# Moving the high and low parts of the weights by 16 and 48 bytes in SBUF

## The reference

```
proj = hn @ w_in[l]
h = h + jnp.concatenate([o_attn, o_rec], axis=-1) @ w_out[l]
g, u = jnp.split(hn @ w_gu[l], [D_FF], axis=-1)
h = h + (jax.nn.silu(g) * u) @ w_down[l]
```

## Time and profile before

| | |
|---|---|
| time, median of 3 runs | 1700.67 us (1699.19 to 1701.57) |
| span of the profiled execution | 1705.6 us |
| mean granted TensorE clock in it | 0.982 |
| TensorE busy | 1619.8 us, 95% |
| weight loads busy (beside TensorE) | 1418.1 us, 83% |
| VectorE busy | 1017.1 us, 60% |
| ScalarE busy | 869.4 us, 51% |
| moved by DMA | 253.94 MB, mean 149 GB/s |

### The profile page before, as it was taken

One profiled execution on the slowest core, in us unless ns is written; L12 is line 12 of the kernel. 1 busy time (PEld: TensorE's weight loads), 2 busy tenths in 40 slices (PEclk: granted clock), 3 DMA queues, 4 the chain that ended last, 5 costly groups with the idle time before them and its releaser, 6 DMA issues.

```text
span 1705.6 us, 28040 instructions
## 1 busy us (share of the span) xinstructions
PE 1619.8 (95%) x11794; PEld 1418.1 (83%) x11794; DVE 1017.1 (60%) x1577; ACT 869.4 (51%) x1467; POOL 21.1 (1%) x38
## 2 busy tenths in 40 slices
PE   6999999989989999999989999999999898999997
PEld 6968999989779999887758778888888674789997
DVE  7675545465855455725465765425556776687676
ACT  6754434448545344534565553324444647666563
POOL 0000000000000000310000000000000000000000
PEclk9999999999999999999999999999999999999999
DMA  7365445353555463772201452232213520154532
GB/s 295 135 231 217 169 152 200 137 194 139 201 214 205 147 232 130 221 229 78 74 1 70 178 198 101 85 128 95 83 68 133 198 100 25 73 208 156 220 144 92
DMA packets 60524, 253.94 MB, mean 149 GB/s; under 512 B 4976, under 2 KB 8304, under 8 KB 42480
## 3 DMA queue, kind: packets, MB, share of 16 engines
q1 hardware_dynamic: 59088, 249.01, 39.6%
q0 software_dynamic: 1312, 3.15, 1.0%
HBM read 251.09 MB, written 1.05 MB: 148 GB/s over the span
## 4 chain that ended last, share of the span: by engine, by line
PE 83%; DVE 9%; ACT 6%; issue 2%; DMA 1%; SPq 0%; DVEq 0%; ACTq 0%
PE PA L910 63%; PE PA L970 4%; DVE WL_t L1550 2%; PE PB L851 2%; PE PB L1320 2%; PE PA L998 2%; PE PB L1307 1%; ACT WH_t L2277 1%; PE PA L946 1%; PE PA L947 1%; PE PA L952 1%; PE PA L865 1%; PE PA L1504 1%; PE PB L1250 1%; DMA raw<-in_w_ada 1%
## 5 line engine op out<-in xcount | busy, mean ns | idle before, releaser
L910 PE MATMUL PA<-XH_t,WH_t 128*128 128x256 f32 (+2 forms) x1984 | 629.6, 317 | 4.9 <-DVE XL_t L1746 2.4
L1550 DVE TENSOR_TENSOR WL_t<-raw,WH_t 128x1024 fp32r<-128x1024 f32 (+1 forms) x344 | 444.5, 1297 | 312.0 <-ACT WH_t L2277 311.6
L910 PE MATMUL PA<-XL_t,WH_t 128*128 128x256 f32 (+2 forms) x1984 | 624.1, 315 | 0.0
L910 PE MATMUL PA<-XH_t,WL_t 128*128 128x256 f32 (+2 forms) x1984 | 623.8, 314 | 0.0
L2277 ACT ACTIVATE WH_t<-raw 128x1024 fp32r<-128x1024 f32 (+1 forms) x344 | 380.8, 1111 | 155.2 <-PE PA L910 139.7
L910 PEld LDWEIGHTS PA<-XH_t,WH_t 128*128 128x128 f32 x1984 | 376.8, 190 | 34.5 <-issue 7.9
L910 PEld LDWEIGHTS PA<-XH_t,WL_t 128*128 128x128 f32 x1984 | 376.9, 190 | 21.6
L910 PEld LDWEIGHTS PA<-XL_t,WH_t 128*128 128x128 f32 x1984 | 377.2, 190 | 21.2 <-issue 0.5
L910 PE MATMUL PA<-AH_t,WH_t 128*128 128x256 f32 (+2 forms) x616 | 192.0, 312 | 0.3 <-DVE AL_t L1596 0.2
L910 PE MATMUL PA<-AH_t,WL_t 128*128 128x256 f32 (+2 forms) x616 | 190.9, 310 | 0.0
L910 PE MATMUL PA<-AL_t,WH_t 128*128 128x256 f32 (+2 forms) x616 | 190.3, 309 | 0.0
(11 more groups left out here) (277 smaller groups left out, 1706.9 us busy)
## 6 DMA issues: line engine op xcount, KB each, us to landing
raw<-in_w_ada SPq DMA_DIRECT2D x48, 1024.0 KB, 5.0
raw<-in_w_gu SPq DMA_DIRECT2D x44, 1024.0 KB, 4.8
raw<-in_w_dn SPq DMA_DIRECT2D x64, 704.0 KB, 4.0
raw<-in_w_up SPq DMA_DIRECT2D x44, 1024.0 KB, 4.8
raw<-in_w_in SPq DMA_DIRECT2D x30, 1024.0 KB, 4.9
raw<-in_w_out SPq DMA_DIRECT2D x12, 1024.0 KB, 4.7
raw<-in_w_qkv SPq DMA_DIRECT2D x6, 1024.0 KB, 5.1
raw<-in_w_outc SPq DMA_DIRECT2D x4, 1024.0 KB, 4.8
```

Source lines behind the costliest of these rows:

```text
L910: mm = pe.matmul(PA[:, (L.b0 + o) % 4, 0:T], W[:, c:c + P], X[:, k, L.x0:L.x0 + T], start=(n == 0 and m == 0 and not L.early), stop=(n == ...
L1550: dve.tensor_tensor(WL_t[:, w:w + L.cols], RAWV[:, r % RAW, part * UNIT:part * UNIT + L.cols], WHf[:, w:w + L.cols], ALU.subtract).then_in ...
```

## The change

`WH_t` and `WL_t` become views into buffers that are 8 columns (32 bytes) longer and begin 4 columns (16 bytes) inside them. `small` becomes 16 columns (64 bytes) shorter; its columns in use end at 46. Loops, instructions, waits and transfers stay as they are.

```diff
--- before.py
+++ after.py
@@ -152,14 +152,16 @@
         XH_t = sb("XH_t", KD * 512, F32R)
         XL_t = sb("XL_t", KD * 512, F32R)
         raw = sb("raw", RAW * CH)
-        WH_t = sb("WH_t", 2 * CH, F32R)
-        WL_t = sb("WL_t", 2 * CH, F32R)
+        WH_at, WL_at = 4, 4
+        WH_b = sb("WH_t", 2 * CH + 8, F32R)
+        WL_b = sb("WL_t", 2 * CH + 8, F32R)
+        WH_t, WL_t = WH_b[:, WH_at:WH_at + 2 * CH], WL_b[:, WL_at:WL_at + 2 * CH]
         Y = sb("Y", 4096)
         tmp = sb("tmp", 5120)
         cboth = sb("cboth", 384)
         cphase = sb("cphase", 2048)
         par = sb("par", NPARAM)
-        small = sb("small", 64)
+        small = sb("small", 48)
         ada = sb("ada", 2 * 96)
         mod = sb("mod", 2 * 2 * 40)
         sc = sb("sc", 40)
@@ -181,7 +183,7 @@
         XH, XL = tiles(XH_t, 0, KD, 512), tiles(XL_t, 0, KD, 512)
         XHf = tiles(XH_t.bitcast(F32), 0, KD, 512)
         RAWV = tiles(raw, 0, RAW, CH)
-        WHf = WH_t.bitcast(F32)
+        WHf = WH_b.bitcast(F32)[:, WH_at:WH_at + 2 * CH]
         AH, AL = tiles(AH_t, 0, FH, 512), tiles(AL_t, 0, FH, 512)
         AHf = tiles(AH_t.bitcast(F32), 0, FH, 512)
         YV = tiles(Y, 0, KD, 512)
```

## The result

| | before | after |
|---|---|---|
| time, median of 20 runs each | 1701.12 us (1699.19 to 1707.91) | 1707.80 us (1699.65 to 1712.25) |
| ratio after / before | | 1.0027, 95% interval 1.0015 to 1.0038 |
| profiled execution: span, mean granted clock | 1705.6 us, 0.982 | 1704.1 us, 0.984 |

A forecast was written before the change was run, and what follows sets the result against it. TensorE's steps, mainly the dense products of L910, were taken to bound the kernel. The terms -6.3 (T = 256) and -1.3 (T = 272), the rest 0, summed to -7.6 us, from 1700.7 to 1693.1 us; range 1660 to 1710 us.

The forecast's parts named there:

- splits: VectorE and ScalarE writing WL_t and WH_t at shifted offsets: taken as 0, covered by TensorE, +2 us at most.
- the move of Y to par: Y to par shift by 64 bytes against rows X and A: counted as 0, with 1 us either way.
- the two reads run into each other: Reading of the traced paces: next weight load and present moving rows collide in memory, in a pattern set by start offsets.
- The first rival: No change, 1700.7 us: something else in the stage sets the pace, or the pattern settles at the same 13.3 ns; chance 0.18.
- Steps with X, T = 512: 1632 steps with rows XH_t, XL_t moving, T = 512: pace of distance 0 kept, 0 us; bounds -11.1 and +3.4.
- the upper bound of +3.4: Dear end for the T = 512 steps with rows XH_t, XL_t: 1632 x 2.1 = +3.4 us.
- T = 256 with X: Steps with rows XH_t, XL_t at T = 256: 120.0 falls to 117.8 ns, 2880 at 2.2 ns, -6.3 us; bounds -19.3 and +6.0.
- T = 272: Steps with rows XH_t, XL_t at T = 272: the half counted as slow goes to 125.6 ns, 1080 x 1.2 = -1.3 us.
- Steps with A: Steps with hidden rows AH_t, AL_t moving, weights taken at distances 80 and 112: 0 us; bounds -13 and +3.3.
- the lower bounds: Cheapest case per step: columns plus 6.7 ns, from the 113.3 ns row; -19.3 us at T = 256 with rows XH_t, XL_t.
- the second rival: Deeper relief: steps fall to columns plus 6.7 ns, 1676 us for T = 256 alone, 1643 for all shapes; chance 0.26.
- The third rival: Slower: distances not multiples of 64 cost 2.1 ns on three kinds of step, 10.2 us, time 1711 us; chance 0.22.

The follow-up runs named there:

- the 64 pairs: TensorE alone repeating the L910 triple, 48 steps per pair of byte distances of WH_t and WL_t from the rows; 226.7 to 235.5 ns at T = 512.
- The steps alone: Programs of TensorE's L910 steps only, other engines idle, sweeping the weights' distances from the rows; at T = 512, (0, 0) gives 226.7 ns and (16, 48) 233.3.

## Why the prediction was wrong

It was right that the places of weights and rows set the pace, and with it what bounds the kernel, the number of steps, that a change of pace lands on the path in full, and that splits, waits and the move of Y to par cost nothing. That the two reads run into each other was a reading, and no run shows it. The first rival, no change, fell: the time per step depends on the offset with every other engine idle, 226.7 to 235.5 ns at T = 512. The Trainium skill, page "TensorE: Matmul & The Clock Gate", section "Step-by-step: what each phase is for", says that loading the next weights takes no read bandwidth from the running matmul. That the offset could not matter was the prediction's conclusion from it, and the 226.7 to 235.5 ns speak against it. What lies behind the two read ports that it names, no run can tell.

The step that failed is "Steps with X, T = 512. The rows give 226.8 at 0 and 228.9 at 64, and 16 and 48 lie between. I take the nearer, distance 0: 0 us". It was +10.1 us, three times the upper bound of +3.4 that I set it. Three things were wrong in it. I treated the pace as a smooth function of the distance, so that 16 and 48 would lie between the values at 0 and 64; it jumps, from 226.7 ns at 0 bytes to 232.5 at 4 and 226.7 again at 16. I took the worst surplus that the trace happened to show, 2.1 ns, as the bound for distances that it did not show. And the row for 64 was not one for 64: counted modulo 256 it is one for 192 (and the distances of A after the change are 208 and 240, not 80 and 112), while both weights 64 bytes above the rows give 233.3. The trace had two distances at T = 512 and no third; that is too few for a bound on two new ones.

Point by point: T = 256 with X, forecast 2880 x 2.2 = -6.3, measured -5.5: right in size, but from the row that was taken for another distance. That was luck of a likely kind, since half of the 64 pairs lie at 118.2 ns or below. T = 272, forecast -1.3, measured -1.7: right, but by a choice that no row decides, so by luck; the 64 pairs lie between 122.2 and 127.4 ns. Steps with A, forecast 0, measured +0.1 - 0.5 + 1.2 = +0.8: within its bounds. T = 512 with X, forecast 0, measured +10.1: wrong, and it makes 10.1 of the 11.2 us between -7.6 and +3.6.

One sign stood in the rows and was not used: a single distance had two paces, 125.6 and 126.8 at T = 272. So a pace read in one stage was not yet the pace of its distance. And the 113.3 ns of the earlier trace rows, the source of the lower bounds and of the second rival, do not come from "these very loads": the 16 steps are of L946 and L947, which use the high weights alone, with no low weights in between. The value does occur with all three products, though, as with both weights 64 bytes on.

The third rival named the direction that won, but spread the cost over three kinds of step at 2.1 ns each, and gave as its reason distances that are no multiple of 64; both weights 64 bytes on cost as much at T = 512, 233.3 ns. In fact T = 512 with X paid 6.2 ns, T = 272 with X gained 0.8 and T = 256 with A paid 0.2, and the total at equal clock is 1701.1 + 3.9 = 1705 us and not its 1711. The surplus over the columns, from which it was to decide, went to 233.2 - 213.3 = 19.9 ns at T = 512 with X; over all 8928 steps it went only from 13.0 to 13.4 ns.

What stays open: why the pace depends on the distance. A collision of the two read streams in SBUF would fit, but no run looks inside, and I have no rule that gives the pace of a distance. Open too is what decides which of its paces a stretch of steps takes: 226.7, 228.9 or 233.3 ns for 16 with 0 and 226.7 or 233.3 for 16 with 16 (T = 512), 113.3 or 117.8 for 64 with 64 (T = 256). The steps alone showed one of them each time. Whether the paces repeat over 256 bytes or over a longer stretch was not tried.

## What to carry to other kernels

Where every matmul has its own weight load, read the distance between starts and set it against T / 2.4 GHz: the rest, here 6.7 to 24 ns a step, depends on where weights and moving rows begin in SBUF. Don't interpolate between offsets, and don't carry one from one T to another; measure a sweep of TensorE's steps alone, and confirm in the whole kernel, stage by stage, since one offset can settle in different paces. If different T want different offsets, shift the moving rows inside their tiles by stage, rather than the weights for all.

## What I had not expected

- A shift of both weights by 4 bytes matters nearly as much as one by 64: from 226.7 to 232.5 and to 233.3 ns at T = 512.
- The same kernel with the same offsets runs the end of one stage at 226.7 ns and the whole of the next but one at 233.3 (T = 512, WH alone moved).
- The surplus over the columns is between 6.7 ns (T = 256 at distances 52, 76 and 88, 113.3 ns) and 24 ns (T = 512 at 164, 237.6 ns). Distance 0, the one that a plain allocation gives here, is among the best of 64 at T = 512 and among the slow ones at T = 256.
- The time of this kernel goes with the mean granted clock run by run, from 0.980 at 1710.7 us to 0.991 at 1699.7 in the changed kernel: a spread that is wider than the effect of the change.
